# Hybrid encoder layer on one core: attention steps moved along the product clock, norm sums moved into the last products, the final scaling divided anew

## What is computed

```python
h = rmsnorm(x, g1)
z = h @ w_in                      # 1024 x (10 * 512 + 8 + 3 * 1024)
(mq, mk, mv, mo, mi, mf, sb, sc, sx, dq, dk, dv, gt) = split(z)
ya = sigmoid(mo) * rmsnorm(mlstm(mq, mk, mv, mi, mf))       # A, 4 heads of 128
yb = sb * causal_dwconv(sc * sx)                            # B, 512 channels
o  = diff_attend(dq, dk, dv, lam, mask)                     # C, 4 heads, block-causal
yc = rmsnorm(o, da_g) * (1 - lam_init)
x  = x + sum_b(sigmoid(gt[b]) * (y_b @ w_branch[b])) @ w_out
h2 = rmsnorm(x, g2)
up = causal_dwconv(h2 @ w_up)                               # 1024 x 2 * 2816
x  = x + (silu(up[:2816]) * up[2816:]) @ w_dn
y  = rmsnorm(x, norm_f)

def diff_attend(q, k, v, lam, mask):      # q, k in two halves of 64 per head
    s = q . k;  p = softmax(s);  return (p[0] - lam * p[1]) @ v
```

## Time and profile before

| | |
|---|---|
| median of 3 runs | 1000.32 us (999.03, 1000.32, 1001.5) |
| the profiled execution | 1000.77 us, its span 999.0 us |
| mean granted clock of TensorE | 0.996 |
| busy: TensorE | 975.5 us, 98% of the span |
| busy: VectorE | 692.0 us, 69% |
| busy: ScalarE | 473.0 us, 47% |
| busy: GpSimd | 161.2 us, 16% |

### The profile page before, as it was taken

One profiled execution on the slowest core, in us unless ns is written; L12 is line 12 of the kernel. 1 busy time (PEld: TensorE's weight loads), 2 busy tenths in 40 slices (PEclk: granted clock), 3 DMA queues, 4 the chain that ended last, 5 costly groups with the idle time before them and its releaser, 6 DMA issues.

```text
span 999.0 us, 20129 instructions
## 1 busy us (share of the span) xinstructions
PE 975.5 (98%) x7763; PEld 952.6 (95%) x7763; DVE 692.0 (69%) x1161; ACT 473.0 (47%) x982; POOL 161.2 (16%) x343
## 2 busy tenths in 40 slices
PE   7999999999999998999999999999999999999996
PEld 6999899999999998999999999999999999999996
DVE  6887666687667898777775547777777777533353
ACT  5675555576555665655553433333333333322241
POOL 2000121110121221121112211111121111111000
PEclk9999999999999999999999999999999999999998
DMA  6522243364231222233244222222222223323342
GB/s 196 196 85 86 77 107 108 99 212 126 64 86 49 80 86 85 65 97 95 80 142 144 85 73 93 89 85 86 85 85 86 85 85 101 117 83 86 90 132 90
DMA packets 104086, 99.87 MB, mean 100 GB/s; under 512 B 4868, under 2 KB 99481, under 8 KB 103735
## 3 DMA queue, kind: packets, MB, share of 16 engines
q1 hardware_dynamic: 98799, 85.51, 28.0%
q10 hardware_dynamic: 4072, 10.23, 2.9%
q0 software_dynamic: 1120, 2.86, 1.0%
HBM read 91.26 MB, written 7.31 MB: 99 GB/s over the span
## 4 chain that ended last, share of the span: by engine, by line
PE 85%; DVE 6%; issue 4%; ACT 4%; POOL 1%; DMA 0%; DVEq 0%; POOLq 0%; ACTq 0%
PE D L1719 46%; PE D L1776 28%; PE D L1736 2%; DVE w_l L1305 2%; ACT w_h L1009 1%; PE X L1988 1%; PE X L2026 1%; PE D L1828 1%; PE D L1748 1%; DVE ups L1675 1%; PE D L1880 1%; PE X L1934 1%; DVE acc L1685 0%; PE X L1935 0%; PE X L1937 0%
## 5 line engine op out<-in xcount | busy, mean ns | idle before, releaser
L1305 DVE TENSOR_TENSOR w_l<-raw,w_h 128x512 fp32r<-128x512 f32 (+1 forms) x286 | 201.0, 720 | 111.2 <-ACT w_h L1009 109.4
L1776 PE MATMUL D<-a_h,w_h 128*128 128x272 f32 x840 | 250.4, 298 | 3.0 <-DVE tmp L1486 1.6
L1776 PE MATMUL D<-a_h,w_l 128*128 128x272 f32 x840 | 243.0, 289 | 0.0
L1776 PE MATMUL D<-a_l,w_h 128*128 128x272 f32 x840 | 241.6, 288 | 0.0
L1009 ACT ACTIVATE w_h<-raw 128x512 fp32r<-128x512 f32 (+1 forms) x286 | 171.5, 618 | 101.0 <-PE D L1719 77.8
L1776 PEld LDWEIGHTS D<-a_h,w_h 128*128 128x128 f32 x840 | 158.1, 188 | 8.4 <-DVE tmp L1486 3.0
L1776 PEld LDWEIGHTS D<-a_l,w_h 128*128 128x128 f32 x840 | 158.4, 189 | 0.0
L1776 PEld LDWEIGHTS D<-a_h,w_l 128*128 128x128 f32 x840 | 158.0, 188 | 0.0
L1719 PE MATMUL D<-h_h,w_h 128*128 128x272 f32 x704 | 145.9, 288 | 0.1
L1719 PE MATMUL D<-h_h,w_l 128*128 128x272 f32 x704 | 145.7, 288 | 0.0
L1719 PE MATMUL D<-h_l,w_h 128*128 128x272 f32 x704 | 145.1, 288 | 0.0
(11 more groups left out here) (346 smaller groups left out, 1676.8 us busy)
## 6 DMA issues: line engine op xcount, KB each, us to landing
raw<-in_w_in SPq DMA_DIRECT2D x64, 512.0 KB, 4.3
raw<-in_w_up SPq DMA_DIRECT2D x44, 512.0 KB, 4.3
raw<-in_w_down SPq DMA_DIRECT2D x20, 512.0 KB, 3.8
raw<-in_w_branch SPq DMA_DIRECT2D x12, 512.0 KB, 3.6
raw<-in_w_out SPq DMA_DIRECT2D x8, 512.0 KB, 4.2
raw<-in_w_down SPq DMA_DIRECT2D x10, 384.0 KB, 3.4
x_spill<-xT ACTq DMA_DIRECT2D x1, 2176.0 KB, 7.4
xT<-x_spill ACTq DMA_DIRECT2D x1, 2176.0 KB, 10.5
```

The lines of the kernel that those rows point to most:

```text
L1305: v.tensor_tensor(split_view(w_l, g), whole_view(g), split_view(w_h, g).bitcast(F32), ALU.subtract)\
L1776: last = t.matmul(out, wt[:, k, :], x[:, left, k, :], start=w in (1, 2, 5) and k == i == 0, stop=k == KQ - 1 and i == 2, skip_group_check= ...
```

## The change

Three things are changed. First, the table of times of the attention: the transposes `t` and their copy `wt` come one product later after their scores (6.5 and 7.5, before 5.5 and 6.5), so do `o`, `sq`, `rr`, `on`, and `y`, `yt`, `yc`; the blocks of the third head start 0, 6, 13 and 21 products after the head's start (before 0, 5, 11, 18), and the fourth head starts at 187 (before 183). Second, `mean 0` and `mean 1` on TensorE no longer stand alone between `dnh 6 1` and `dnh 7 1`; they are issued inside `dnh 6 1` and `dnh 7 1`, behind half of the weight tiles of each (`mean_of_halves`). Third, in the final scaling VectorE takes the second half of token block 3, ScalarE the first half of the channels of the sample rows, and the transfer of the sample rows is issued by ScalarE's queue.

```diff
@@ -135,9 +135,10 @@
                        (92, ("sample", "ex", 1))):
         at_time(time, *step)
     for u in range(17):
-        t0, t1 = (99 + 28 * (x // 4) + (0, 5, 11, 18)[x % 4] if x >= 0 else 91 for x in (u - 1, u))
-        for dt, sub in ((0, "s"), (1, "mx"), (2, "ex"), (3, "wd"), (5.5, "t"), (6.5, "wt"), (8, "o"), (9, "sq"),
-                        (9, "rr"), (11.5, "on"), (t1 - t0 + 8, "y"), (t1 - t0 + 9, "yt"), (t1 - t0 + 9, "yc")):
+        t0, t1 = ((99, 127, 155, 187, 215)[x // 4] + ((0, 5, 11, 18), (0, 6, 13, 21))[x // 4 == 2][x % 4] if x >= 0 else 91
+                  for x in (u - 1, u))
+        for dt, sub in ((0, "s"), (1, "mx"), (2, "ex"), (3, "wd"), (6.5, "t"), (7.5, "wt"), (9, "o"), (10, "sq"),
+                        (10, "rr"), (12.5, "on"), (t1 - t0 + 9, "y"), (t1 - t0 + 10, "yt"), (t1 - t0 + 10, "yc")):
             if u or dt > 2:
                 at_time(t0 + dt, "at", sub, u)
 
@@ -229,9 +230,9 @@
     unit("mean", 0)
     unit("yTh", KD - 1, 0)
     unit("yTh", KD - 2, 1)
-    unit("mean", 1)
     unit("scale", 0)
     add("dnh", KD - 1, 1)
+    unit("mean", 1)
     unit("yTh", KD - 1, 1)
     unit("mean", 2)
     unit("scale", 1)
@@ -779,11 +780,9 @@
                     .then_inc(raw_in[i % NRAW], 16)
 
             for i, (c, cols) in enumerate(((0, slice(0, DM)), (1, slice(0, DM)), (2, slice(0, DM // 2)),
-                                           (2, slice(DM // 2, DM)))):
+                                           (2, slice(DM // 2, DM)), (3, slice(DM // 2, DM)))):
                 sp.wait_ge(S["y_dve"], i + 1)
                 sp.dma_start(y_p[0, P * c:P * c + P, cols], yst[:, c, cols]).then_inc(S["y_out"], 16)
-            sp.wait_ge(S["y_dve"], 5)
-            sp.dma_start(y_s[0], yst_s[0:TS, :]).then_inc(S["y_out"], 16)
             sp.wait_ge(S["y_out"], 7 * 16)
             sp.wait_ge(S["out_k"], 64)
             sp.wait_ge(S["out_v"], 64)
@@ -1105,12 +1104,15 @@
                 elif kind == "scale" and a[0] == 1:
                     act.wait_ge(S["rs_ready"], 3)
                     act.wait_ge(S["y_copied"], KD + 2)
-                    for i in range(2):
-                        cols = slice(DM // 2 * i, DM // 2 * (i + 1))
-                        sc.activation(yst[:, 3, cols], yst[:, 3, cols], ACT.Copy, scale=ssx[:, 3:4])\
-                            .then_inc(S["y_act"], 1)
-                        act.wait_ge(S["y_act"], i + 1)
-                        act.dma_start(y_p[0, 3 * P:4 * P, cols], yst[:, 3, cols]).then_inc(S["y_out"], 16)
+                    cols = slice(0, DM // 2)
+                    sc.activation(yst[:, 3, cols], yst[:, 3, cols], ACT.Copy, scale=ssx[:, 3:4]).then_inc(S["y_act"], 1)
+                    sc.activation(yst_s[0:TS, cols], yst_s[0:TS, cols], ACT.Copy, scale=ssx[0:TS, 4:5])\
+                        .then_inc(S["y_act"], 1)
+                    act.wait_ge(S["y_act"], 1)
+                    act.dma_start(y_p[0, 3 * P:4 * P, cols], yst[:, 3, cols]).then_inc(S["y_out"], 16)
+                    act.wait_ge(S["y_act"], 2)
+                    act.wait_ge(S["y_dve"], 6)
+                    act.dma_start(y_s[0], yst_s[0:TS, :]).then_inc(S["y_out"], 16)
                 elif kind == "p" and a[1] in (1, 6, 7, 4):
                     q, w = a
                     blk, half = {1: (0, 0), 6: (1, 0), 7: (1, 1), 4: (0, 1)}[w]
@@ -1454,11 +1456,13 @@
                     dve.wait_ge(S["rs_ready"], 2 + a[0])
                     dve.wait_ge(S["y_copied"], KD + 2 * a[0])
                     for c, cols in ((0, slice(0, DM)), (1, slice(0, DM))) if a[0] == 0 else \
-                            ((2, slice(0, DM // 2)), (2, slice(DM // 2, DM))):
+                            ((2, slice(0, DM // 2)), (2, slice(DM // 2, DM)), (3, slice(DM // 2, DM))):
                         v.tensor_scalar(yst[:, c, cols], yst[:, c, cols], ssx[:, c:c + 1], None, ALU.mult)\
                             .then_inc(S["y_dve"], 1)
                     if a[0]:
-                        v.tensor_scalar(yst_s[0:TS], yst_s[0:TS], ssx[0:TS, 4:5], None, ALU.mult).then_inc(S["y_dve"], 1)
+                        cols = slice(DM // 2, DM)
+                        v.tensor_scalar(yst_s[0:TS, cols], yst_s[0:TS, cols], ssx[0:TS, 4:5], None, ALU.mult)\
+                            .then_inc(S["y_dve"], 1)
                 elif kind in ("yT", "yTh"):
                     j, x = a[0], 2 * (a[0] % 2)
                     dve.wait_ge(S["y_tr"], y_event[(kind, *a)] + 1)
@@ -1791,6 +1795,19 @@
                     last = t.matmul(out[0:L, c:c + 1], src[:, col:col + L], mean_w[:, 0:1], start=True, stop=True)
                 last.then_inc(S["norm_mm"], 1)
 
+            def mean_of_halves(part):
+
+                pe.wait_ge(S["sq_added"], KD - 1 + KD - 2)
+                pe.wait_ge(S["sq_done"], KD + KD - 2 + 2 + (part + 1 if part else 0) - (part > 0))
+                out = D[:, (1, 3, 1)[part], :]
+                for c in HALF_TILES[min(part, 1)]:
+                    col, L = TILES[c]
+                    for i in ((0, 1, 2), (0, 1), (2,))[part]:
+                        source = (ssum[2][:], tmp_of(("sq", 2, KD - 2)), tmp_of(("sq", 2, KD - 1)))[i]
+                        last = t.matmul(out[0:L, c:c + 1], source[:, col:col + L], mean_w[:, 0:1],
+                                        start=i in (0, 2 * (part // 2)), stop=i == (2, 1, 2)[part])
+                last.then_inc(S["norm_mm"], 1)
+
             def spread_rstd(out, before, tiles):
                 for i, c in enumerate(tiles):
                     L = TILES[c][1]
@@ -1833,18 +1850,8 @@
                     for m in waits_of[block_of[("if",)]]:
                         wait_drained(pe, m)
                     turn_over(9, banks(block_of[("if",)])[:, 0, :])
-                elif kind == "mean":
-
-                    pe.wait_ge(S["sq_added"], KD - 1 + KD - 2)
-                    pe.wait_ge(S["sq_done"], KD + KD - 2 + 2 + (a[0] + 1 if a[0] else 0) - (a[0] > 0))
-                    out = D[:, (1, 3, 1)[a[0]], :]
-                    for c in HALF_TILES[min(a[0], 1)]:
-                        col, L = TILES[c]
-                        for i in ((0, 1, 2), (0, 1), (2,))[a[0]]:
-                            source = (ssum[2][:], tmp_of(("sq", 2, KD - 2)), tmp_of(("sq", 2, KD - 1)))[i]
-                            last = t.matmul(out[0:L, c:c + 1], source[:, col:col + L], mean_w[:, 0:1],
-                                            start=i in (0, 2 * (a[0] // 2)), stop=i == (2, 1, 2)[a[0]])
-                    last.then_inc(S["norm_mm"], 1)
+                elif kind == "mean" and a[0] == 2:
+                    mean_of_halves(2)
                 elif kind == "mk" and a[0] == 0:
                     gates_and_first_key(block_of[("if",)], n)
                 elif kind == "mk":
@@ -1868,7 +1875,8 @@
                 elif kind == "dn":
                     product(n, g_h, g_l, (lambda k: pe.wait_ge(S["gl_ready"], k + 1)) if a[0] == 0 else None)
                 elif kind == "dnh":
-                    product(n, g_h, g_l, halves=(a[1],), at_bank=0)
+                    half_means = (lambda k: mean_of_halves(a[0] - (KD - 2)) if k == JF // 2 else None) if a[1] else None
+                    product(n, g_h, g_l, half_means, halves=(a[1],), at_bank=0)
                 elif kind in ("tok", "tokS"):
                     name, j = a[0]
                     if kind == "tok":
```

## The result

| | before | changed |
|---|---|---|
| median | 999.61 us (6 runs, 998.58 to 1001.5) | 1004.26 us (6 runs, 1002.97 to 1004.9) |
| ratio, 95% interval | 1 | 1.0041 (1.0029 to 1.0053) |
| profiled execution, its span | 1000.77, 999.0 us | 1002.97, 1001.2 us |

I forecast 999.4 us, 0.9 us less than before. The change costs 4.1 us by the ratio. The profiled pair shows 2.2 of it: the profile before is above its median, the profile after is the lowest run of its kernel. The rest is taken up with the second profiles (experiment 8).

A forecast was written before the change was run, and what follows sets the result against it. TensorE, busy 98%, was taken as the bound, so only its waits and slow clock could be won. +2.7 - 1.9 - 1.4 - 0.3 = -0.9 us from the 1000.32 median gave 999.4 us, range 995.6 to 1002.6.

The forecast's parts named there:

- the sum of the late heads: Attention stretch to 405 us: old waits won less two new waits, -1.9 us in all, bounds -6.4 to +1.5.
- the new wait: TensorE before `y` of unit 9, on `wdT` from unit 10's `wt`, now behind ScalarE's drain: 3.5 us.
- the old waits: Seven TensorE waits in 330 to 410 us, 5.0 us together, 6.4 with restarts, taken as won.
- the wait for unit 11 (1.0 us): Second new wait on ScalarE's `wdT`, for `wt` of unit 11 in the late heads, taken as 1.0 us.
- the 0.2 us for each restart: Late heads: each of seven TensorE waits also costs 0.2 us from start to start, making 5.0 into 6.4 us.
- Rival (b): VectorE sets the late-head stretch; only 2 of 6.4 us won, new waits cost 5: 1004.3 us, chance 0.12.
- Unit 0, +2.7 us: First head: `s` of unit 1 waits 1.7 us for the copy `wt`, `pr 0 1` 1.0 us for write-back.
- The clock, -1.4 us: End of kernel: sums inside the products remove the light stretch and the clock fall in `dnh 7 1`, winning 1.4 us.
- only five transposes are left: Between `dnh 6 1` and `dnh 7 1`: with the sums moved inside, no light stretch remains ahead of a clock fall.
- Rival (c): The clock fall is not in most runs, or stays; 1.4 us drops out of the sum: 1000.8 us, chance 0.18.
- The scaling, -0.3 us: Final scaling: the last issue comes at about 994.55 instead of 994.83, 0.3 us earlier; bounds -0.8 and 0.
- `pr 2 0`: Later `yc` of unit 16 could hold up `pr 2 0`; forecast no cost, slack left over 1 us.

The follow-up runs named there:

- experiment 8: Second profiles of unmodified kernels: the changed kernel again, 1004.40 us, and the kernel before again, 1001.97 us.
- experiment 2: Changed kernel with the attention's unit 0 at its old times, all other units at the new ones: 1001.40 us, ratio 1.0012 to the kernel before.
- the distances alone: Kernel before with `t`, `wt`, `o` and the rest one product later for all units but unit 0, old head and block starts: 999.35 us, ratio 0.9990.
- experiment 6: Kernel before with the norm sums inside the last products, and the five transposes moved inside `dnh 7 1`: 999.49 us, ratio 0.9988.
- `wt` ahead: Changed kernel with unit 0 at its old times and the copy `wt` of every other unit one product earlier: 998.69 us, ratio 0.9985.
- the last two of experiment 9: Changed kernel, unit 0's old times, VectorE's `lo` two products earlier: with `wt` earlier and transposes inside `dnh 7 1`, 996.95 us; with neither, 999.76 us.
- experiment 3: Changed kernel with VectorE's step `lo` of both sb pairs (`yb_l`) two products earlier: 1002.50 us, ratio 1.0013 to the kernel before.
- the first of 9: Changed kernel with unit 0 at its old times, other units' `wt` one product earlier, five transposes inside `dnh 7 1`: 997.67 us, ratio 0.9968.
- the fastest kernel: Changed kernel with unit 0's old times, `wt` one product earlier, transposes inside `dnh 7 1`, VectorE's `lo` two products earlier: 996.95 us, ratio 0.9960.

## Why the prediction was wrong

- **The step that failed is the sum of the late heads**, "-6.4 + 3.5 + 1.0 = -1.9 us". Measured: 0.45 us longer in the changed kernel's first profile and 1.5 in its second; the ratios, less the other terms, give 0.9 (table alone) to 2.1 (changed kernel), each with about 1 us of uncertainty. What failed above all is the price of the new wait. It was found and nearly sized, 3.86 for 3.5; but I priced it at its duration, and the clock at half speed behind it cost 1.5 us more in one profile and 2.7 in the other. Second, the old waits were booked as wholly won, but two waits for drains (0.6 and 0.5 us) stand in their place. Third, the wait for unit 11 (1.0 us) didn't come. With the 0.2 us for each restart, waits of 5.0 us in three places instead of seven give -0.8, and with the fall of 1.5 it is +0.7, beside the +0.45 of the profile.
- **Rival (b)** named 1004.3 us, and 1004.26 was measured. That is luck: it held that only 2 of the 6.4 us are won and that the waits for units 10 and 11 cost 5.0, and it has no clock in it. In the profile 4.9 of the 6.4 are won (two waits for drains, 1.1 us, and their restarts remain), and what outweighs it is one new wait and the clock behind it.
- **Unit 0, +2.7 us**, was right: 1.59 and 0.95 us of waits in the trace, 2.87 us from start to start. That experiment 2 gives 2.9 by the ratios is in part chance, since 1.0 of it is taken back at unit 1 in its profile.
- **The clock, -1.4 us**, was right in its mechanism as far as the profiles tell: without the light stretch there is no fall. The profiles with the sums outside show the fall near 980 us in five of six (both profiles of before, the table alone, the scaling alone, the distances alone; not the new starts alone), those with the sums inside in none of eleven. The size was off. The fall costs 1.53 us, but "only five transposes are left" between the products, and these wait for VectorE's drain, 0.7 us, which had been behind `mean 0`; the sums inside the products take 0.2 us more than alone. So 0.65 us are won where there was a fall and 0.88 lost where there was none, as in the 29 of 99 runs of before that seem to have none. Over all runs -0.4 us (-1.3 to +0.4) was measured, and -1.2 with the wait hidden (experiment 6). Rival (c), that the fall is not in most runs, was thus right for a part of the runs. The rule for the price in the Trainium skill, "TensorE: Matmul & The Clock Gate", section Terms, gives an estimate of 1.5 us for a fall of 3 us at one half, beside the 1.46 us from start to start. Its Part 1 says that the moment of a transition varies from run to run; the two profiles of the changed kernel agree, where behind the same wait the clock is back at 1.00 at about 389 us in one and at 392 in the other.
- **The scaling, -0.3 us**: 0.16 us in the trace from the first scaling to the last issue, nothing that the runs can tell.
- **`pr 2 0`** cost nothing: no wait for `yc` is in the profile of the changed kernel. The slack was smaller than forecast: the last write of `yc_l` ended at 483.86 and the first matmul of `pr 2 0` began at 484.37.
- **Slips that changed nothing**: the light stretch before the fall holds 29 matmuls, 24 records of the sums and 5 transposes, and not 32, since three of `dnh 6 1` reach into the window; and the sums are not 18 matmuls.

What stays open is why a wait of about 2 us brings the clock down in some profiles (the new starts alone, `wt` ahead, the last two of experiment 9) and not in others (experiment 3, the first of 9). With one profile of each, it may be chance or the kernel. Behind 3.9 us it fell in all four that have it (the changed kernel twice, the table alone, unit 0's old times).

## What to carry to other kernels

Where a copy moves to a later place on an in-order engine, look what that engine waits for just ahead of it: two shifts that are harmless alone put `wt` behind a drain that waits for another engine's last piece, and the consumer is one product away. In a stretch in which VectorE is 90% busy, don't book a wait of TensorE as won because its cause is gone: it can return at another place. The sum of the waits from 330 to 410 us was 5.0 us before and after the change, 4.1 with the distances alone and 2.7 in the fastest kernel, whose VectorE does the same work in another order; so it isn't fixed either, and it is the sum that has to be forecast. And a wait of TensorE of some microseconds has two prices, its duration and the clock behind it.

## What the runs showed of the hardware

The granted clock of a single core fell from 1.00 to 0.50 in three places: behind idle waits of 1.8 to 3.9 us, in eight of the ten profiles that have one between 378 and 389 us; behind 29 light matmuls in 3 us (five profiles of six); and in two of seventeen profiles near 114 us, behind 24 small products of the mLSTM in 3.8 us. A fall lasted about 3 us, or 6 in one profile. Each 3 us cost 1.5 us. The runs of the kernel before lie in three groups by their mean clock, at 999.1, 1000.9 and 1001.9 us in the mean, which most likely are those with none, one and two falls.
